# Hybrid attention, RWKV-7 and MoE layer on one core: y rows read back without the last two experts' scatters, and empty expert slots that gather a row

## What is computed

```python
def route(xf, w_router, b_router):
    s = jax.nn.sigmoid((xf @ w_router).astype(jnp.float32))
    sel = s + b_router.astype(jnp.float32)
    grp = jnp.sum(lax.top_k(sel.reshape(-1, N_EXPERT_GROUPS, EXPERTS_PER_GROUP), 2)[0], -1)
...
    _, e_idx = lax.top_k(jnp.where(in_grp, sel, NEG_INF), TOP_K)
    w = jnp.take_along_axis(s, e_idx, axis=-1)
    return e_idx, w / jnp.sum(w, -1, keepdims=True)
...
    def expert_block(args):
        xb, e = args
        h = jax.nn.silu(xb @ w_gate[e]) * (xb @ w_up[e])
        return h @ w_down[e]
...
        x = layer_norm(DEEPNORM_ALPHA * x + y.reshape(B, S, D), ln_g[l, 2], ln_b[l, 2])
```

## Time and profile before

| | us |
|---|---|
| median of 3 runs | 1140.33 |
| lowest, highest | 1139.0, 1142.72 |
| span of the profiled execution | 1135.4 |
| PE busy | 1058.4 (93%) |
| DVE, ACT, POOL busy | 345.5, 273.6, 85.8 |

### The profile page before, as it was taken

How to read it: one execution, slowest core, us unless ns; L and a number is a source line. 1 busy time by engine, 2 the same in 40 slices (tenths; PEclk the granted TensorE clock), 3 DMA queues, 4 the chain that set the end, 5 groups by cost and what they waited for, 6 DMA issues and landing times.

```text
span 1135.4 us, 15981 instructions
## 1 busy us (share of the span) xinstructions
PE 1058.4 (93%) x6710; PEld 533.3 (47%) x6710; DVE 345.5 (30%) x729; ACT 273.6 (24%) x540; POOL 85.8 (8%) x133
## 2 busy tenths in 40 slices
PE   9999999999899999999998999999998898898896
PEld 4444455566655544566446544444443333333332
DVE  0179522334664453104146211111111011011116
ACT  2431122234454500023202211222111011011123
POOL 2000100000000000100000211111111101101110
PEclk9999999999999999999999899999999989989999
DMA  8112220222024320923316999999999999999996
GB/s 278 37 41 86 97 76 2 76 76 76 14 64 149 110 77 1 361 84 117 148 74 257 368 398 404 403 394 393 393 396 392 401 395 394 399 396 401 398 401 251
DMA packets 55847, 263.31 MB, mean 232 GB/s; under 512 B 7250, under 2 KB 8402, under 8 KB 30944
## 3 DMA queue, kind: packets, MB, share of 16 engines
q1 hardware_dynamic: 49424, 252.81, 57.8%
q0 software_dynamic: 5120, 8.40, 2.3%
q10 hardware_dynamic: 1232, 1.07, 0.3%
HBM read 257.60 MB, written 13.05 MB: 238 GB/s over the span
## 4 chain that ended last, share of the span: by engine, by line
PE 31%; DMA 24%; DVE 3%; issue 1%; ACT 1%; SPq 0%; POOLq 0%; ACTq 0%; DVEq 0%
DMA ring<-in_w_exp_up 7%; PE cpair L2020 5%; PE bank L2030 5%; PE tpair L2020 4%; DMA ar<-in_w_exp_up 3%; PE bank L1861 2%; PE bank L1841 2%; DMA mixT<-in_w_exp_down 2%; DMA ring<-in_w_exp_down 2%; DMA avq<-in_w_exp_up 2%; PE tpair L1861 1%; PE bank L1834 1%; PE cpair L1861 1%; PE tpair L1841 1%; PE cpair L1841 1%; DMA mixT<-y_rows 1%
## 5 line engine op out<-in xcount | busy, mean ns | idle before, releaser
L2020 PE MATMUL cpair<-ring,xgT 128*64 128x512 f32 x312 | 82.8, 594 | 7.6 <-DMA ring<-in_w_exp_up 4.4
L2234 ACT ACTIVATE hs<-cpair 64x512 f32<-64x512 f32 x21 | 12.4, 589 | 237.7 <-PE cpair L2020 237.7
L2464 DVE SCALAR_TENSOR_TENSOR ye<-bank,tabs,xgt 128x512 f32<-128x512 f32 x30 | 22.5, 751 | 136.0 <-PE bank L2030 136.0
L2030 PE MATMUL bank<-ring,hT 128*64 128x512 f32 x224 | 57.6, 656 | 6.2 <-DVE hT L2454 6.2
L2450 DVE TENSOR_TENSOR hs<-cpair,hs 64x512 f32<-64x512 f32 x21 | 14.6, 693 | 154.3 <-ACT hs L2234 154.3
L922 PE MATMUL bank<-xT,ring 128*128 128x512 f32 x128 | 60.9, 606 | 0.0
L1776 POOL DMA_INDIRECT y_rows<-ye,tabs x30 | 30.3, 1011 | 383.8 <-DVE ye L2464 383.8
L2020 PEld LDWEIGHTS cpair<-ring,xgT 128*64 128x64 f32 x312 | 26.2, 137 | 53.1 <-issue 52.0
L365 PE MATMUL bank<-xT,ring 128*128 128x512 f32 x112 | 48.5, 593 | 0.0
L2241 ACT ACTIVATE xgt<-xgt,tabs 64x512 f32<-64x512 f32 x64 | 46.0, 719 | 1.6
L2020 PE MATMUL tpair<-ring,xgT 128*64 128x512 f32 x152 | 39.5, 594 | 4.5 <-DMA ring<-in_w_exp_up 2.5
(11 more groups left out here) (471 smaller groups left out, 1894.7 us busy)
## 6 DMA issues: line engine op xcount, KB each, us to landing
ring<-in_w_exp_gate SPq DMA_DIRECT2D x30, 1024.0 KB, 11.1
ring<-in_w_exp_down SPq DMA_DIRECT2D x30, 1024.0 KB, 11.1
ring<-in_w_exp_up SPq DMA_DIRECT2D x28, 1024.0 KB, 11.2
ring<-in_w_in SPq DMA_DIRECT2D x6, 2048.0 KB, 8.1
ring<-in_w_mem_kv SPq DMA_DIRECT2D x4, 2048.0 KB, 10.3
mixT<-in_w_exp_down SPq DMA_DIRECT2D x7, 1024.0 KB, 10.3
ar<-in_w_exp_down SPq DMA_DIRECT2D x7, 1024.0 KB, 11.0
xT<-in_w_exp_gate SPq DMA_DIRECT2D x6, 1024.0 KB, 11.5
```

Source lines behind the costliest of these rows:

```text
L2020: last = nc.tensor.matmul(bank[b][m * CAP:(m + 1) * CAP, :], xgT[:, k, :], w(m, h)[:, j * DE:(j + 1) * DE], start=(k == 0), stop=(k == KT ...
L2030: last = nc.tensor.matmul(bank[b][m * CAP:(m + 1) * CAP, :], ht[:, k, :], w(2, h)[:, o:o + 512], start=(k == 0), stop=(k == FT - 1))
```

## The change

It has two parts.

**Empty slots.** `tokens_read` adds `spread` to the number of each slot that is empty (`vacant`): slot p of expert e then names token 8 p + e mod 8, so the gather fetches a real row for it. Its gate and its target row are as before, so the scatter skips it. (In the loop over further blocks the same, on tables of its own, `tabs2`.)

**The end.** `y_rows` is set to zero by one DMA of 4.19 MB, issued by SP behind weight piece 7, from a part of `xgt` that POOL zeroes first. Experts 30 and 31 get gate and ALPHA x in `ye` by DVE like all the others, and `combT` holds ones (`last_oh`) instead of gates; so their ALPHA x need not be scattered, and the two last scatters go, with `late_out` and SP's wait for it. Their tokens are turned and copied in the loop or right after it, expert 31's into a place of its own (`xgT_last`). On PE the first four matmuls of the combination stand ahead of `down(31)`. Some of the places used at the end are renumbered.

```diff
-        def tokens_read(dve, n):
+        def tokens_read(dve, tabs, ls, n):
             dve.wait_ge(tab_full, 2 * n - 1)
-            nc.vector.tensor_scalar(tabs[0:CAP, :, 0], bank[6][0:CAP, 0:NE], float(OFF), None, ALU.add).then_inc(tokens_known, 1)
+            nc.vector.scalar_tensor_tensor(ls.vacant[0:CAP, :], bank[6][0:CAP, 0:NE], 0.0, spread[0:CAP, :], ALU.is_ge, ALU.mult)\
+                .then_inc(vacant_known, 1)
+            dve.wait_ge(vacant_known, n)
+            nc.vector.scalar_tensor_tensor(tabs[0:CAP, :, 0], bank[6][0:CAP, 0:NE], float(OFF), ls.vacant[0:CAP, :], ALU.add,
+                                           ALU.add).then_inc(tokens_known, 1)
...
+                    sp.wait_ge(zero_here, 1)
+                    sp.dma_start(y_rows.rearrange("(r p) c -> p r c", p=P),
+                                 xgt[:, 0, 0:512].unsqueeze(1).to_broadcast([P, 2 * TOP_K * S // P, D // 2]))\
+                        .then_inc(rows_cleared, 16)
...
                     rows_out(sp)
-                    sp.wait_ge(late_out, 32)
                     down_read(sp, LAST - 2)
...
+                    pool.memset(xgt[:, 0, 0:512], 0.0).then_inc(zero_here, 1)
+                    pool.wait_ge(zero_here, 1)
...
+                    link(pool, pool.iota(spread[:, :], pattern=[[0, NE // KT], [1, KT]], base=-OFF, channel_multiplier=KT,
+                                         allow_small_or_imprecise_dtypes=True))
...
-                    for e in PE_LAST:
-                        pool.wait_ge(x_done, 2 * (e + 1))
-                        scatter(tabs[:, e, 1:2], xrow[:, e % 2, :]).then_inc(late_out, 16)
...
-                        if e + 1 < LAST - 1:
-                            tokens(e + 1)
+                        tokens(e + 1)
                         hidden(e)
                         down(e)
+                    pe.wait_ge(xgt_read, LAST)
+                    tokens(LAST)
...
                     e, f = PE_LAST
-                    tokens(e)
                     gate_up(e, 0)
                     gate_up(e, 1)
-                    tokens(f)
                     gate_up(f, 0)
                     hidden(e)
                     gate_up(f, 1)
                     down(e)
                     hidden(f)
-                    down(f)
...
                     combined(0, 0, True)
                     combined(1, 0, True)
+                    down(f)
...
-                    def unscaled(e):
-                        act.wait_ge(y_out[e % 2], 16 * (LAST - 1) // 2)
-                        down_read(act, e)
-                        nc.scalar.activation(ye[:, e % 2, :], bank[5 if e < LAST else 0][:, :], ACT.Copy)\
-                            .then_inc(y_scaled, 1)
...
+                    link(dve, V.tensor_copy(last_oh[:, :, :, :], oh[:, 0:TOP_K, :, LAST - 1:NE]))
...
-                    for e in PE_LAST:
-                        hidden(e)
-                        turned(e)
+                    e, f = PE_LAST
+                    hidden(e)
+                    turned(e)
+                    hidden(f)
+                    out_rows(e)
+                    turned(f)
+                    out_rows(f)
```

More of the change, by code:

```diff
@@ L1588, in hybrid_decoder_trunk @@
         yb = [free[t].rearrange("p (k d) -> p k d", k=TOP_K) for t in range(NT)]
-        ob = [free[NT + t // 2][:, (t % 2) * D:(t % 2 + 1) * D] for t in range(NT)]
-        ln3 = free[6].rearrange("p (h d) -> p h d", h=2)
-        spare = free[7].rearrange("p (b d) -> p b d", b=2)
+        xgT_last = free[4][:, 0:KT * CAP].rearrange("p (k c) -> p k c", k=KT)
+        xgT2 = free[4][:, 512:512 + KT * CAP].rearrange("p (k c) -> p k c", k=KT)
+        xrow2, tabs2 = free[4][:, 1024:1536], free[4][:, 1536:1536 + 4 * NE].bitcast(I32).rearrange("p (e f) -> p e f", f=4)
+        ob = [free[5 + t // 2][:, (t % 2) * D:(t % 2 + 1) * D] for t in range(NT)]
+        ln3 = free[9].rearrange("p (h d) -> p h d", h=2)
+        spare = free[10].rearrange("p (b d) -> p b d", b=2)
         x3 = [yb[t][:, 0, :] for t in range(NT)]
-        further_piece = lambda i, h: free[2 * i + h]
-        xf = free[6][:, 0:D]
-        ls2 = Lists(free[8])
+        further_piece = lambda i, h: free[(0, 1, 2, 3, 5, 6)[2 * i + h]]
+        ls2 = Lists(free[7])
+        xf = free[8][:, 0:D]
         acc = ((6, 7), (3, 1), (2, 4), (5, 0))
@@ L2019, in gate_up_terms @@
                             for m in both:
-                                last = nc.tensor.matmul(bank[b][m * CAP:(m + 1) * CAP, :], xgT[:, k, :],
+                                last = nc.tensor.matmul(bank[b][m * CAP:(m + 1) * CAP, :], xt[:, k, :],
                                                         w(m, h)[:, j * DE:(j + 1) * DE],
@@ L2041, in gate_up @@
                             piece_here(pe, number[e, i, h])
-                        gate_up_terms(1 + e % 3, lambda i, h: piece(e, i, h), h).then_inc(w_read, 1)
+                        gate_up_terms(1 + e % 3, xgT if e < LAST else xgT_last, lambda i, h: piece(e, i, h), h).then_inc(w_read, 1)
                     def hidden(e):
@@ L2201, in tokens @@
                         act.wait_ge(t2_full, b + 1)
+                        if b == 1:
+                            act.wait_ge(rows_cleared, 16)
                         nc.scalar.activation(x2T[hf][:, :, t * P:(t + 1) * P],
@@ L2228, in tokens @@
                         act.wait_ge(xgt_full, e + 1)
-                        nc.scalar.activation(xgT[:, :, :].rearrange("p k c -> p (k c)"), bank[0][:, :], ACT.Copy)\
+                        if e == LAST:
+                            down_read(act, LAST - 3)
+                        to = xgT if e < LAST else xgT_last
+                        nc.scalar.activation(to[:, :, :].rearrange("p k c -> p (k c)"), bank[0][:, :], ACT.Copy)\
                             .then_inc(xgt_read, 1)
@@ L2257, in experts @@
                                 nc.scalar.activation(combT[:, a, :], bank[6 + a][:, :], ACT.Copy).then_inc(comb_read, 1)
-                        if e + 1 < LAST - 1:
-                            tokens(e + 1)
-                            first_rows(e + 1)
+                        tokens(e + 1)
+                        first_rows(e + 1)
+                    tokens(LAST)
+                    first_rows(LAST)
                     def before():
@@ L2268, in body @@
                             act.wait_ge(f_t, g)
-                            nc.scalar.activation(xgT[:, :, :].rearrange("p k c -> p (k c)"), bank[0][:, :], ACT.Copy)\
+                            nc.scalar.activation(xgT2[:, :, :].rearrange("p k c -> p (k c)"), bank[0][:, :], ACT.Copy)\
                                 .then_inc(f_xt, 1)
@@ L2272, in body @@
                             for h in range(2):
-                                nc.scalar.activation(xrow[half[h], 0, :], xf[half[0], h * 512:(h + 1) * 512], ACT.Copy,
+                                nc.scalar.activation(xrow2[half[h], :], xf[half[0], h * 512:(h + 1) * 512], ACT.Copy,
                                                      scale=coefc[half[0], :]).then_inc(f_xr, 1)
@@ L2287, in experts @@
                     act.wait_ge(set_done, 1)
-                    nc.scalar.activation(nmean[:, 0:1], eps[:, :], ACT.Sqrt)
-                    unscaled(e)
-                    unscaled(f)
+                    nc.scalar.activation(blkones[:, 62:63], eps[:, :], ACT.Sqrt)
                     for t in range(NT):
```

47 lines of the change are left out of this document (24 added, 23 removed).

## The result

The kernel after takes 1159.14 us (median of 4 runs, 1157.4 to 1160.39), the kernel before 1141.53 us in the runs beside it (median of 4, 1139.0 to 1142.79): 17.6 us more by the medians. The ratio of the runs is 1.0163, 95% interval 1.0143 to 1.0183, which is 18.6 us (16.3 to 20.9). Slower was forecast with 0.90, and the time lies in the range; the forecast of 1166.5 was 7.4 us too high. The profiled execution took 1157.4 us, 1.9 over its span.

The account below looks back on a forecast made before the run. Bound by saturated DMA engines streaming weights (share 1.01, 640 to 1104 us). Terms +27.6 + 0.5 - 0.7 - 1.2 = +26.2 us on the 1135.4 us span give 1161.6; with 4.9 us carried over, 1166.5 us, range 1149 to 1175.

Parts of the forecast that it names:

- A: Rival on the gathers: an added row costs only its bytes, 9.7 ns; +8.6 us, 1149 us; chance 0.12.
- B: Rival on the gathers: rows into half of the partitions go at half rate, 19.5 ns each; 1158.8 us; chance 0.18.
- C: The forecast's own case on the gathers: 24 to 33 ns a row, 1163 to 1173 us; chance 0.52.
- Empty slots: Step 1, gathers in the saturated weight stream: 1024 more rows at 27 ns each, +27.6 us.
- Routing: Step 2, token column before the first gather: two DVE instructions with a semaphore replace one; +0.5 us, between 0 and 1.5.
- Two scatters: Step 3, scatters of experts 30 and 31 go: 56 rows at 12.7 ns, -0.7 us.
- Readback early: Step 4, first readback on SP: issued 4.8 us earlier but behind four pieces; -1.2 us, bounds 0 and 4.8.
- Clearing: Step 5, zeroing y_rows (4.19 MB) in 510 to 575 us, hidden by idle engines: 0; 10 to 13 us without cover.
- The order at the end: Step 6, expert 31's scaled copy on DVE and four combination matmuls ahead of down(31): both fall into waits, 0.
- D: Rival on the gathers: full gathers with evenly spaced rows cost 36 ns or more a row; 1176 us or more; chance 0.08.
- F: Rival on the slots: filling one is free since its packet already exists; -1.4 us, 1138.9 us; chance 0.03.
- E: Rival on the weight stream: added rows only fill SP's waits for PE; -5.0 us, 1135.3 us; chance 0.07.

Follow-up runs that it names:

- g_half: Kernel before, one weight place fewer, one more unread gather per loop expert, 64 rows of 4096 B into partitions 0 to 63: 1191.86 us, +50.2 over g_skip.
- e_down_first: Kernel after, with PE's down(31) put back ahead of the four combination matmuls that need only expert 30: 1159.05 us, ratio 1.0168 to the kernel before.
- g_skip: Kernel before, one weight place fewer, one more unread gather per loop expert, all 64 indices out of bounds: 1141.7 us.
- experiments 4 and 5: Kernel before with extra unread gathers into varied partitions, 1141.7 to 1191.86 us; then its own gathers over all partitions, new end, 1118.67 us, slots filled 1124.77.
- g_mid: Kernel before, one weight place fewer, one more unread gather per loop expert, 64 rows into partitions 32 to 95: 1161.1 us, +19.4 over g_skip.
- experiment 6: Kernel after with added rows close together in memory, 1159.99 us; kernel after with empty slots skipped and the y_rows clearing issued twice, 1139.63 us (once: 1138.67).

## Why the prediction was right, and where it was off

The bound was read rightly: weights with a share of 1.01, and what is added to their stream is paid in time. The size was 7.4 us too high. Of that, 1.3 us come from the 4.9 us between span and median that I carried over: after the change it is 3.6, of which 1.9 us are around the span of the profiled execution and the rest is spread. The other 6.1 us are in the span, which grew by 20.1 us (1.7 of them ahead of the change) instead of 26.2. The time is in the range because the range reached down to A for the sake of A and B; C's own 1163 to 1173 doesn't hold it. The steps:

1. **Empty slots.** +27.6 forecast, +18.4 by the run with this part alone. This is the step that failed, and in one factor: the price of one more row, 27 ns taken, 17.6 (times) to 18.9 (queues) measured. The range of 24 to 33 ns did not hold it. For a gather as it now is, 27 was nearly right: in the 28 stretches of 9 us around a gather and a scatter the weights are short by 2.07 us on average; less 33 scattered rows at 12.7 ns, 1.65 us are left for 64 gathered ones, 26 ns each, as in g_half. I had given 355 to 370 GB/s for such a stretch whatever the expert; they lie at 355 to 382, mean 369. But the gathers before, half as full, cost more than half of that. So what the added rows cost is less than the average price (below).
2. **Routing.** +0.5 forecast. PE's first transpose of the experts moves from 631.27 to 633.35 us, 0.4 us beyond the shift of 1.7. Right.
3. **Two scatters.** -0.7 forecast. The software queue has 160 packets fewer; the time isn't told apart from step 4's, the two together gave -1.1 (-2.4 to +0.1) where I had -1.9.
4. **Readback early.** It is issued 1.5 us after the last weight piece (before 5.1), and DVE ends 0.7 us sooner after that piece, not 1.2. In e_down_first `mixT` takes 16.57 us from its issue instead of 13.1: as forecast, the early issue mostly waits behind the pieces in flight.
5. **Clearing: 0.** Right as far as the runs can tell: a second clearing costs about 1 us (3 at most).
6. **The order at the end: 0.** Nearly right. The row sums did wait for expert 31's scaled copy, which I had expected to end before the second row pair lands; it costs 0.3 to 0.4 us.
7. **The last part.** 14.8 us before and after.

**What the price per row was worth.** The rows before can be taken apart further than I did. In the kernel after every gather has 64 rows, so its software queue tells how many rows each scatter has, and with that how many each gather before had. My pair is 36 scattered and 18 gathered rows against 44 and 55: 37 of the 45 added rows are gathered ones, 27 ns each. Two more stretches of the kernel before, 870 to 879 us (36 scattered, 39 gathered):

```profile
q1 hardware_dynamic: 412, 3.01, 90.7%
q0 software_dynamic: 160, 0.30, 10.6%
```

and 955.3 to 964.3 us (44 scattered, 31 gathered):

```profile
q1 hardware_dynamic: 448, 3.28, 91.8%
q0 software_dynamic: 160, 0.30, 9.8%
```

Against the earlier trace rows 21 gathered rows more cost 0.28 MB of weights, 32 ns each; against the earlier trace rows 24 fewer gave back 0.45 MB, 45 ns each. A least-squares fit over all 28 stretches from 655 to 1080 us, with gathers of 18 to 55 rows, gives 28 ns for a gathered row (standard error 3), 10 for a scattered one (3) and 0.2 us besides. So within the sizes seen the slope was 27 or more, no smaller than an average, and hardly a fixed part: the skipped gathers of g_skip allow 0.1 us each. What failed is that I continued the line beyond them. In four traces with skipped slots such a stretch is short by 1.41 us, in four with filled ones by 2.10: 0.69 us for 31 rows, 22 ns each. And 3 us of the rest were hidden where I had put nothing: SP's waits for PE were 12.0 us before (4.4 and 4.1 in the earlier trace rows, 3.5 in one row more) and 9.0 after. 1024 rows at 22 ns less 3 us are 19.5 us; measured are 18.0. The hiding is argued from the waits, no run shows it by itself.

Of the rivals, **B (1158.8, 0.18)** came nearest. Its cause is shown by experiments 4 and 5: the half of the partitions, not the row. Its price is not: no gather in the traces costs 19.5 ns a row, a full one costs 26, and that the time came out within 0.4 us of B's is in part luck. The rule of the Trainium skill, page "SBUF — State Buffer", section "Door 1: The DMA port swizzle (why `[64,N]` ≈ `[32,N]`)", that I had weighed against my rows spoke for a lower price than my rows, and for its direction I had only compared gathers with scatters; the placement of the price was open, and it was what mattered. A (bytes), D (steeper, spacing) and F (free) fell. E (slack) fell as a whole, but its mechanism took about 3 of the 27.6 us, by the waits above.

Open: why a full gather costs more than half rate (26 against 19.5 ns), and why the price flattens at the top: the one gather of 55 rows cost no less than one of 64. No run varied the number of rows in one gather with all else equal.

## What to carry to other kernels

Beside a stream that fills the DMA engines, ask of every transfer not only how many bytes it has but which partitions it touches: 64 rows into partitions 0 to 63 cost 1.67 us, the same rows into 32 to 95 cost 0.65 us. A price for more of the same holds for the sizes from which it was read: gathers of 18 to 55 rows gave 28 ns a row, and the step from half full to full cost 22 in the stream and 18 in the time, so a forecast beyond the sizes seen needs a wider range or a run at the new size. And a limit that a reordering removes is worth only the distance to the next one: measure where that stands (here 0.3 to 0.4 us behind) before counting a queue position as gain.

## What the runs showed of the hardware that I had not expected

- A transfer into half of the partitions slows everything beside it: one of 0.26 MB took 1.67 us out of a stream of 421 GB/s, more than the 1.25 us it would have at half of that rate. The total rate over 420 us fell from 396 to 373 GB/s (g_skip to g_half) and stayed at 397 in g_mid.
- With gathers over all partitions the engines average 416 GB/s (slots skipped) and 419 (filled) over 660 to 1080 us, gathers, scatters and code loads included, against 397 before (166.93 MB in 420 us).
- A 4.19 MB fill of DRAM from one small tile, issued behind two weight pieces, cost about 1 us of the 10 it takes by bytes, no more than the runs can tell from nothing (experiment 6).
